# 16 instead of 32 key columns for the meta tokens, and a ring of five split weight blocks instead of four

## The reference

```python
h = jnp.concatenate([meta (16 rows), x (256 rows), zeros], axis=1)
xn = rmsnorm(h, norm_mix_g)
sb_q, sb_k, sb_v, df_q, df_k, df_v = jnp.split(xn @ w_in, splits, axis=-1)   # 1024 columns each
# stick-breaking attention, 8 heads of 128
z = q @ k.T * 128 ** -0.5;  u = where(causal, log_sigmoid(-z), 0)
a = where(causal, exp(log_sigmoid(z) + (cumsum from the right of u) - u), 0);  o_sb = a @ v
# differential attention, 8 heads of 2 x 64
s = q @ k.T * 64 ** -0.5 - slope * |qpos - kpos|;  p = softmax(where(mask, s, -inf))
o_df = rmsnorm((p[:, :, 0] - lam * p[:, :, 1]) @ v, subln_g) * 0.2
merged = gate0 * (o_sb @ w_br_sb) + gate1 * (o_df @ w_br_df);  h = h + merged @ w_out
h = h + (silu(hn @ w_ffn_gate) * (hn @ w_ffn_up)) @ w_ffn_down;  y = rmsnorm(h, norm_final_g)
```

## Time and profile before

| | |
|---|---|
| time, median of 3 runs | 800.6 us (800.35 to 801.55) |
| the profiled execution, its own time | 800.49 us |
| its span, first to last instruction | 798.6 us |
| mean granted clock of PE | 0.996 |
| PE busy | 778.0 us (97%) |
| DVE busy, ACT busy | 550.3 us (69%), 424.4 us (53%) |
| chain that ended last | PE 89%, DVE 5%, ACT 2% |
| a 1 MB chunk of `w_in`, issue to landing | 5.2 us |

### The profile page before, as it was taken

One profiled execution on the slowest core, in us unless ns is written; L12 is line 12 of the kernel. 1 busy time (PEld: TensorE's weight loads), 2 busy tenths in 40 slices (PEclk: granted clock), 3 DMA queues, 4 the chain that ended last, 5 costly groups with the idle time before them and its releaser, 6 DMA issues.

```text
span 798.6 us, 13449 instructions
## 1 busy us (share of the span) xinstructions
PE 778.0 (97%) x5250; PEld 680.4 (85%) x5250; DVE 550.3 (69%) x913; ACT 424.4 (53%) x832; POOL 108.4 (14%) x105
## 2 busy tenths in 40 slices
PE   7999999999998999999999999999999999999996
PEld 4788988788897878999977998999987888888885
DVE  6897977857987573447547577877866656666665
ACT  5447548845547553547347455664444545454453
POOL 1334015501625120000000000101001000000000
PEclk9999999999999999999999999999999999999999
DMA  8856311144533433843415634335655556555641
GB/s 298 227 168 212 106 54 54 54 156 144 158 106 107 131 107 108 267 154 118 146 54 173 197 121 144 106 106 185 208 167 176 189 172 223 194 176 174 219 135 53
DMA packets 93106, 120.76 MB, mean 151 GB/s; under 512 B 8490, under 2 KB 69347, under 8 KB 93044
## 3 DMA queue, kind: packets, MB, share of 16 engines
q1 hardware_dynamic: 92176, 117.68, 45.5%
q0 software_dynamic: 432, 1.57, 0.6%
q10 hardware_dynamic: 436, 0.65, 0.2%
HBM read 118.85 MB, written 1.05 MB: 150 GB/s over the span
## 4 chain that ended last, share of the span: by engine, by line
PE 89%; DVE 5%; ACT 2%; issue 1%; POOL 1%; DMA 1%; ACTq 0%; POOLq 0%; DVEq 0%
PE banks L448 21%; PE banks L450 20%; PE banks L449 20%; PE banks L500 8%; PE banks L502 4%; DVE w_lo L1678 1%; PE banks L1081 1%; PE banks L640 1%; PE banks L558 1%; PE banks L520 1%; PE banks L594 1%; PE banks L606 1%; PE banks L684 1%; ACT tmp L1372 1%; DMA cst<-in_c_keep 1%
## 5 line engine op out<-in xcount | busy, mean ns | idle before, releaser
L1678 DVE TENSOR_TENSOR w_lo<-raw,w_hi 128x1024 fp32r<-128x1024 f32 x210 | 261.7, 1255 | 102.5 <-ACT w_hi L1232 101.9
L1232 ACT CAST w_hi<-raw 128x1024 fp32r<-128x1024 f32 (+1 forms) x211 | 219.0, 1047 | 154.1 <-PE banks L450 120.3
L448 PE MATMUL banks<-h,w_hi 128*128 128x256 f32 (+1 forms) x512 | 149.6, 292 | 0.3 <-DVE w_lo L1678 0.3
L449 PE MATMUL banks<-h,w_hi 128*128 128x256 f32 (+1 forms) x512 | 145.4, 284 | 0.0
L450 PE MATMUL banks<-h,w_lo 128*128 128x256 f32 (+1 forms) x512 | 144.8, 283 | 0.0
L448 PE MATMUL banks<-w_hi,h 128*128 128x512 f32 (+1 forms) x264 | 105.3, 399 | 0.8 <-DVE h L1685 0.6
L450 PE MATMUL banks<-w_hi,h 128*128 128x512 f32 (+1 forms) x264 | 102.9, 390 | 0.0
L449 PE MATMUL banks<-w_lo,h 128*128 128x512 f32 (+1 forms) x264 | 102.6, 388 | 0.0
L500 PE MATMUL banks<-h,w_hi 128*128 128x512 f32 x288 | 99.0, 392 | 0.0
L448 PEld LDWEIGHTS banks<-h,w_hi 128*128 128x128 f32 x512 | 96.1, 188 | 2.6 <-issue 2.0
L450 PEld LDWEIGHTS banks<-h,w_lo 128*128 128x128 f32 x512 | 96.5, 189 | 0.0
(11 more groups left out here) (353 smaller groups left out, 1364.7 us busy)
## 6 DMA issues: line engine op xcount, KB each, us to landing
raw<-in_w_in SPq DMA_DIRECT2D x24, 1024.0 KB, 5.2
raw<-in_a_w_in SPq DMA_DIRECT2D x13, 1024.0 KB, 5.2
raw<-in_w_ffn_gate SPq DMA_DIRECT2D x11, 1024.0 KB, 5.4
raw<-in_w_ffn_up SPq DMA_DIRECT2D x11, 1024.0 KB, 5.4
raw<-in_w_ffn_down SPq DMA_DIRECT2D x11, 1024.0 KB, 5.0
raw<-in_b_w_in SPq DMA_DIRECT2D x9, 1024.0 KB, 5.2
raw<-in_w_gate SPq DMA_DIRECT2D x8, 1024.0 KB, 5.3
raw<-in_a_w_out SPq DMA_DIRECT2D x4, 1024.0 KB, 5.1
```

Of the source, the lines that this page charges most:

```text
L448: mm(o, lh, rh, start=start, stop=False)
L449: mm(o, lh, rl, start=False, stop=False)
L1232: nc.scalar.copy(split(w_hi, s), rawsub(s)[0]).then_inc(S["hi_ready"], 1)
L1678: V.tensor_tensor(split(w_lo, s), rawsub(s)[0], split(w_hi, s).bitcast(F), ALU.subtract).then_inc(S["lo_ready"], 1)
```

## The change

The metas stand in `h` once instead of twice: 16 columns for 32. Everything that has the metas' width follows: keys 272 wide for 288, score rows 416 for 448, the second tile at column 144 for 160, and a constant that is 32 columns shorter. `h` has 288 columns for 416 (W_H), which frees 8 KB to a partition, and `RING` goes from 4 to 5, which takes them. Line numbers of the kernel after are one higher than before from the changed constants on.

```diff
-RING = 4
+RING = 5
-COL = (0, P + MP)
-W_H = 2 * P + MP + P
-KEYS = 2 * P + MP
+COL = (0, P + META)
+W_H = 2 * P + 2 * META
+KEYS = 2 * P + META
+DW = 3 * P + 2 * META
...
                 for c in range(2):
-                    mm(ps[2 + c][:, 0:448], isl, dist[:, 0:448], start=True, stop=False)
-                for a, w, q in ((0, 160, 0), (160, 288, P)):
+                    mm(ps[2 + c][:, 0:DW], isl, dist, start=True, stop=False)
+                for a, w, q in ((0, COL[1], 0), (COL[1], KEYS, P)):
...
-                keys = [t[:, :, P:P + MP].rearrange("p a (r n) -> p a r n", n=META) for t in (h_hi, h_lo)]
+                keys = [t[:, :, P:P + META] for t in (h_hi, h_lo)]
...
-                link(V.tensor_copy(keys[0], bc(mt, [P, KT, 2, META], 2)))
-                V.tensor_tensor(keys[1], bc(mt, [P, KT, 2, META], 2), keys[0].bitcast(F), ALU.subtract).then_inc(S["m_h"], 1)
+                link(V.tensor_copy(keys[0], mt))
+                V.tensor_tensor(keys[1], mt, keys[0].bitcast(F), ALU.subtract).then_inc(S["m_h"], 1)
...
             def take_sk(f):
                 split_lo_to(first["sk"] + f + RING)
                 dve.wait_ge(S["sub_used"], first["sk"] + f + 1)
-                V.tensor_copy(skT[:, f, :], ps[SKB[f]][:, 0:KEYS]).then_inc(S["fm_dve"], 1)
+                V.tensor_copy(skT[:, f, 0:KEYS], ps[SKB[f]][:, 0:KEYS]).then_inc(S["fm_dve"], 1)
```

More of the change, by code:

```diff
@@ L37 @@
 RAW = 3
-RING = 4
+RING = 5
 SLOT = 1024
-COL = (0, P + MP)
-W_H = 2 * P + MP + P
-KEYS = 2 * P + MP
+COL = (0, P + META)
+W_H = 2 * P + 2 * META
+KEYS = 2 * P + META
+DW = 3 * P + 2 * META
 C_ID, C_CB, C_CM, C_BM, C_IF, C_END = 0, 128, 160, 192, 200, 232
-G_CAUS, G_PREV, G_TRI, G_BLK, G_ONE, G_DIST, G_END = 0, 128, 256, 384, 512, 640, 1088
+G_CAUS, G_PREV, G_TRI, G_BLK, G_ONE, G_DIST, G_END = 0, 128, 256, 384, 512, 640, 1056
 def shape_constants():
@@ L69, in shape_constants @@
     g[:, G_ONE:G_ONE + P] = -1.0
-    m = np.arange(MP)
+    m = np.arange(META)
     far = lambda seen, dist: np.where(seen, dist, -NEG)
-    dm = lambda tt: far((m[None, :] < META) & (i[:, None] >= 0), np.abs(META + tt * P + i[:, None] - m[None, :]))
+    dm = lambda tt: far((m[None, :] >= 0) & (i[:, None] >= 0), np.abs(META + tt * P + i[:, None] - m[None, :]))
     near = far(i[None, :] // 64 <= i[:, None] // 64, np.abs(i[:, None] - i[None, :]))
-    g[:, G_DIST:G_DIST + 448] = np.concatenate([near, dm(0), P + i[:, None] - i[None, :], dm(1), near], axis=1)
+    g[:, G_DIST:G_DIST + DW] = np.concatenate([near, dm(0), P + i[:, None] - i[None, :], dm(1), near], axis=1)
     return c, g
@@ L210, in program @@
         minus_ones = crr[:, G_ONE - G_TRI:G_ONE - G_TRI + MP].bitcast(F)
-        dist = crr[:, G_DIST - G_TRI:G_DIST - G_TRI + 448]
+        dist = crr[:, G_DIST - G_TRI:G_DIST - G_TRI + DW]
         qr = ar[:, 0:2048].rearrange("p (t n) -> p t n", t=2)
@@ L1089, in d_transposes @@
                 wm = xn[:, 1408 + T * (h % 2):1408 + T * (h % 2) + T]
-                for j, c in enumerate((0, 160, 320)):
+                for j, c in enumerate((0, COL[1], 2 * COL[1])):
                     nc.tensor.transpose(ps[4][:, P * j:P * j + P], w[:, c:c + P], ident)
@@ L1594, in _ @@
                 t = tmp[:, 896 * (h % 2) + 448 * c:896 * (h % 2) + 448 * c + 448]
-                A(t[:, 0:160], b[:, 0:160], ACT.Exp, bias=nmax[:, 2 * u:2 * u + 1], accum_out=sums[:, 2 * u:2 * u + 1]).then_inc(S["act"], 1)
-                A(t[:, 160:448], b[:, 160:448], ACT.Exp, bias=nmax[:, 2 * u + 1:2 * u + 2], accum_out=sums[:, 2 * u + 1:2 * u + 2]).then_inc(S["d_p"], 1)
+                A(t[:, 0:COL[1]], b[:, 0:COL[1]], ACT.Exp, bias=nmax[:, 2 * u:2 * u + 1], accum_out=sums[:, 2 * u:2 * u + 1]).then_inc(S["act"], 1)
+                A(t[:, COL[1]:DW], b[:, COL[1]:DW], ACT.Exp, bias=nmax[:, 2 * u + 1:2 * u + 2], accum_out=sums[:, 2 * u + 1:2 * u + 2]).then_inc(S["d_p"], 1)
                 split_hi_to(first["gate"] + u + RING)
@@ L2126, in take @@
                     dve.wait_ge(S["sub_used"], first["dk"] + i + 1)
-                    V.tensor_copy(dkT[:, i, :], ps[i % 2][:, 0:KEYS]).then_inc(S["fm_dve"], 1)
+                    V.tensor_copy(dkT[:, i, 0:KEYS], ps[i % 2][:, 0:KEYS]).then_inc(S["fm_dve"], 1)
                 elif i < 16:
@@ L2243, in d_max @@
                 b = ps[2 + u % 2]
-                V.tensor_reduce(nmax[:, 2 * u:2 * u + 1], b[:, 0:160], X, ALU.max, negate=True).then_inc(S["dve"], 1)
+                V.tensor_reduce(nmax[:, 2 * u:2 * u + 1], b[:, 0:COL[1]], X, ALU.max, negate=True).then_inc(S["dve"], 1)
                 chain[0] += 1
-                V.tensor_reduce(nmax[:, 2 * u + 1:2 * u + 2], b[:, 160:448], X, ALU.max, negate=True).then_inc(S["d_max"], 1)
+                V.tensor_reduce(nmax[:, 2 * u + 1:2 * u + 2], b[:, COL[1]:DW], X, ALU.max, negate=True).then_inc(S["d_max"], 1)
             def df_variance(h):
@@ L2280, in _ @@
                     link(V.tensor_scalar(rr[:, 2:4], rr[:, 2:4], lam[:, 5:6], None, ALU.mult))
-                    for i, (a, b) in enumerate(((0, 160), (160, 448))):
+                    for i, (a, b) in enumerate(((0, COL[1]), (COL[1], DW))):
                         link(V.tensor_scalar(t1[:, a:b], t1[:, a:b], rr[:, 2 + i:3 + i], None, ALU.mult))
@@ L2284, in _ @@
                         link(last)
-                    metas = t0[:, 0:320].rearrange("p (a n) -> p a n", a=2)[:, :, P:P + META]
+                    metas = t0[:, 0:2 * COL[1]].rearrange("p (a n) -> p a n", a=2)[:, :, P:P + META]
                     V.tensor_scalar(xn[:, 1408 + T * (h % 2):1408 + T * (h % 2) + T].rearrange("p (a r n) -> p a r n", a=2, n=META),
```

## The result

The changed kernel takes 807.3 us (806.9 to 809.1, 4 runs) beside 801.1 for the kernel before; the ratio is 1.0084, 95% interval 1.0072 to 1.0096, so +5.8 to +7.7 us. The direction was forecast. The size was not: the forecast was +3.9, and 807.3 is outside the range's 806.2.

A forecast was written before the change was run, and what follows sets the result against it. PE, busy 97% of the span, was taken as the bound; -2.8 + 0.5 - 0.6 - 0.7 + 4.7 + 1.7 + 1.1 = +3.9 on 800.49 gave 804.4 us (48%, 803.4 to 805.4), with a wider range of 800.4 to 806.2.

The forecast's parts named there:

- narrow keys: Key tiles and d_scores on PE: narrower matmuls, -2.8 + 0.5 - 0.6 = -2.9 us.
- the fifth place where PE waits: PE's two waits for w_lo: splits made one position sooner remove them, -0.7 us.
- the branch products: At br_sb, a second DVE low part ahead of L2305 delays PE's fifth tile: +1.1 us, no clock lost.
- quad 1: ACT's cast of dq+0 waits for chunk 52 before z_exp(1, 2): stall 4.7 us plus clock loss 1.7 us.
- The stall: PE at filler(16) in quad 1 waits for DVE's copies, 5.2 us late less 0.48 slack: +4.7 us.
- The 0.5 given back: At key tile dk+2 PE meets a bank that DVE copies no sooner; slack 0.36 us, so +0.5 us.
- faster: Rival: the late cast in quad 1 is covered, so 4.7 and 1.7 fall away: 798.0 us; chance 14%.
- the stall without the clock: Rival: z_sums cuts up the quad 1 gap and the clock stays up: 802.7 us; chance 17%.
- worse: Rival: the clock falls at 546 as well, or for longer at 436: 806.1 us; chance 9%.
- The clock behind the gap: After PE's 3.7 us idle in quad 1 the clock drops to the lower level: +1.7 us, bounds 0 and 3.4.
- the narrowing: 384 key matmuls at L448, L449 and L450, each 7.3 ns shorter for 16 fewer columns: -2.8 us.
- the scores: d_scores matmuls of L1081 lose 0.43 us and the bias matmuls of L1077 0.2: together -0.6 us.

The follow-up runs named there:

- e2: Narrower keys alone, changed kernel with the ring back at four places: 800.5 us, ratio 0.9994 to the kernel before.
- e4: Changed kernel with the split positions of quad 1 and the low parts at the branch products one block back: 799.5 us, ratio 0.9984.
- e3: Changed kernel with the splits of quad 1 on ACT and DVE back at their old blocks, ring of five kept: 801.1 us, ratio 1.0000.
- e1: The changed kernel measured again, for a second trace: 807.8 us, ratio 1.0087 to the kernel before.
- e14: Changed kernel with the matmuls of z_sums(1, 2) done six times, filling PE's gap in quad 1: 806.0 us, ratio 1.0066.
- e13: Changed kernel with one number changed, ACT's second split of quad 1 ending one block earlier: 806.3 us, ratio 1.0068.
- e5: The kernel before measured again, for a second trace: 800.8 us, ratio 0.9996.
- e12: Kernel before with all of h starting 16 columns further on in its row: 802.7 us, ratio 1.0024.
- e16: Kernel before with all of h starting 32 columns further on in its row: 801.5 us, ratio 1.0010.
- e11: Ring of five, narrow keys, quad 1 and branch product positions back, metas first in h without unused columns in front: 798.2 us, ratio 0.9962.
- e15: Narrow keys, ring of four, metas first in h, 112 unused columns in front, rows of 384: 798.0 us, ratio 0.9974.
- e6: Narrow keys with ring of four, rows of h 416 columns wide again, the added ones unused: 800.3 us, ratio 0.9993.
- e10: Ring of five, narrow keys, quad 1 and branch product positions back, metas first in h behind 16 unused columns: 798.4 us, ratio 0.9969.

## Why the prediction was wrong

By the ratios the change divides into: narrow keys -0.5 (e2), the fifth place where PE waits -0.8 (e4 against e2), the branch products +1.3 (e3 against e4), quad 1 +7.0 (e1 against e3). That is +7.0, e1's own; each is a difference of neighbours, so that the sum has to close. The forecast had -2.9, -0.7, +1.1 and +6.4: of the 3.1 us that it missed, 2.4 are in the first term and 0.6 in the last.

**Right.** The stall: 4.84 us in the trace beside 4.7, at the instruction and for the transfer named, with ACT's wait of about 4 us, DVE's late copies and the late low parts of `z_sums` in it. The branch products: 1.13 in the trace beside 1.1, with no fall of the clock behind. The two weight waits: gone from the trace, 0.8 beside 0.7 by the ratios. The 0.5 given back: at dk+2 the shift grows by 0.5 in e2's trace. The rival "faster" is refuted by the stall itself and by e3, "the stall without the clock" by the stretch at 0.50 shown with e14. Of "worse", the longer fall behind the gap came, at a smaller price.

**Half right.** The clock behind the gap was put at 1.7. Behind `filler(16)` PE's shift grows by 2.3 us in the first trace, 1.7 in e1 and 2.8 in e13; e14 gives 1.7, with about 1.5 to either side. The mechanism is shown. Its size came from one stretch of one trace, and that it was near is partly luck, as the last section shows.

**Wrong, and it is what took the time out of the range.** The step that failed is the narrowing, "384 x 7.3 ns = 2.8 us less" with -0.6 for the scores, taken as all that the new columns of `h` do to PE. The narrowed matmuls gave that much. The mistake was that every other matmul was put at nothing, without a reason. Groups of e2, to be read against the earlier trace rows:

```profile
L449 PE MATMUL banks<-h,w_hi 128*128 128x256 f32 x384 | 111.1, 289 | 0.3 <-DVE w_lo L1679 0.3
L451 PE MATMUL banks<-h,w_lo 128*128 128x256 f32 x384 | 108.4, 282 | 0.0
L450 PE MATMUL banks<-h,w_hi 128*128 128x256 f32 x384 | 108.2, 282 | 0.0
...
L449 PE MATMUL banks<-h,w_hi 128*128 128x272 f32 x128 | 38.0, 297 | 0.3 <-DVE ar L2128 0.3
L451 PE MATMUL banks<-h,w_lo 128*128 128x272 f32 x128 | 37.1, 290 | 0.0
L450 PE MATMUL banks<-h,w_hi 128*128 128x272 f32 x128 | 36.7, 287 | 0.0
...
L1082 PE MATMUL banks<-ar 64*128 64x272 f32 x32 | 5.0, 389 | 0.0
...
L1082 PE MATMUL banks<-ar 64*128 64x144 f32 x32 | 4.1, 335 | 0.0
```

The 272 wide ones last 297 and 290 ns for 303 and 294; over the three lines their busy time falls from 114.2 to 111.8 us, 2.4. L1082 has lost 13 ns per matmul, 0.8 us over its 64, as durations. But the 256 wide matmuls with `h`, whose shape nobody touched, have gone from 107.2 to 108.4 us at the last line alone, and over the three lines from 325.7 to 327.7: 2.0 back. (L449 of the kernel before, which the earlier trace rows leaves out, has 107.7 at 256 columns and 37.8 at 288.) So it goes on in the last block, here e5 (the kernel before) and then e2:

```profile
L450 PE MATMUL banks<-h,w_lo 128*128 128x256 f32 x384 | 107.2, 279 | 0.0
...
L502 PE MATMUL banks<-h,w_lo 128*128 128x256 f32 x252 | 70.1, 278 | 0.0
```

```profile
L503 PE MATMUL banks<-h,w_lo 128*128 128x256 f32 x252 | 70.6, 280 | 0.0
```

Another 0.5. Durations overlap, so the sum goes by steps from start to start, in the first trace of the kernel before and in e2 (both with a clock of 0.83 in 246 to 256). The narrowed key matmuls take 2.7 us less and the scores 0.7 less, as forecast. But the 1456 other 256 wide ones with `h` take 1.9 more, and 1080 more with `h`, nearly all 512 wide, 0.9 more. All the rest comes to 0.0, with the 0.5 of dk+2 in it. That is -0.6, beside the measured -0.5.

What is shown: where the columns of `h` lie changes the time at equal work (e12 and e16 against e5, nothing else moved), and of each of the two kernels both traces have the same last 649 steps to 0.01 us. What is not: which property of the place it is. Start at a multiple of 128 or 512 bytes (e11, e15, e16) and length of the row (e6) are ruled out as the single rule, and which it is stays open. No run tells whether PE's own two streams or other engines' accesses meet there.

## What to carry to other kernels

A deeper ring whose depth also sets positions in in-order queues moves every wait forward, and what counts is the block that is not bound by the ring but by its transfer: look for the chunk with the least time between landing and first use, and for who stands behind that wait. Undoing one position can leave the next to meet the same wait (e13); undo the stretch (e3). Having narrowed a tile, compare the matmuls whose shape did not change, too; in this kernel their 1 to 3 ns each ate most of the gain. A different order of the columns got part of it back: e10 and e11, metas first, are 0.3 to 0.4% under the kernel before, of which e4 had 0.16 without it.

## What the hardware showed that I had not expected

The clock behind one and the same gap isn't one number. Four stretches: 246 to 256 of the first trace of the kernel before, of e5 (the same kernel), and of the changed kernel, then 118 to 122 of e3 (the clock is third from the end):

```profile
246.00:256.00 10.00, 8.09 (x82) 6.67 (x82) 6.09 (x12) 8.13 (x26) 4.08 (x4) 0.83 0.31 106
```

```profile
246.00:256.00 10.00, 7.70 (x90) 6.46 (x90) 7.03 (x13) 8.84 (x30) 4.20 (x5) 1.00 0.31 106
```

```profile
246.00:256.00 10.00, 7.54 (x59) 6.32 (x57) 5.85 (x13) 7.37 (x24) 4.07 (x4) 0.66 0.26 101
```

```profile
118.00:122.00 4.00, 3.31 (x21) 2.65 (x22) 3.68 (x9) 2.38 (x12) 1.91 (x3) 0.57 0.00 0
```

Behind a gap of 2.5 or 2.6 us PE's mean clock over 10 us was 0.83, 1.00 and 0.66, which is 1.7, 0 and 3.4 us of clock lost. Of the 18 traces of this case, 11 are like the first, 3 like the second and 4 like the third. Not all of it is time. Against e5, its own kernel, the first trace is 1.4 us behind at 256 and 0.6 from 264 on, since PE then waits less for POOL (L696, 0.3 us in all for 1.0). The changed kernel is 2.8 us behind at 256 and 1.9 from 264 on.

And behind the 1.3 us wait for POOL at 117, where the kernel before kept its clock at 1.00, e3 ran at 0.57 for 4 us (e10 too, the other 16 traces not). That is 1.7 us of clock, and cost PE 0.5. The prediction took a gap under 1.7 us for safe at the branch products; there the clock held, but this row shows that it need not.

So what a gap costs in clock is drawn anew in each execution, and one trace shows one draw. Two traces of one kernel can differ by 1 to 2 us for it, up to half of this change's whole forecast; the medians of several runs, not the traces, have to settle sums.

The other is the 123.31, 123.82, 123.91, 124.19, 124.29 and 124.52 us for the same 649 steps. In e12 and e16 (124.29, 123.91) nothing differs from the kernel before (123.31) but the columns at which `h` stands.
